# GpSimd's weight split reordered, an earlier opening, and two reorderings between TensorE and VectorE in a four-block model kernel

## What is computed

```
x = x + rmsnorm(mamba2_mixer(rmsnorm(x)))          # in-projection 1024 -> 6176, conv of 4 taps, 8 groups of
                                                   # 4 heads over 4 chunks of 128 tokens, gate, out 2048 -> 1024
x = x + rmsnorm(swa_sink_mixer(rmsnorm(x)))        # 4 key/value heads, window of 128, sinks, gate, out
x = x + conv_pool_mixer(rmsnorm(x)); x = x + swiglu_ffn(rmsnorm(x))
x = x + hgrn2_mixer(rmsnorm(x));     x = x + swiglu_ffn(rmsnorm(x))
out = rmsnorm(x)

# the part of the mamba mixer that the change touches
z, xbc, dt = split(h @ w_in)
xs, B, C   = split(silu(causal_conv(xbc)))
y = ssd(xs, dt, A, B, C) + d_skip * xs
y = rmsnorm(y * silu(z), gate_norm) @ w_out
# and of the attention mixer
o = softmax(...) @ v ;  o = (o * silu(gate)) @ w_out
```

## Time and profile before

| | |
|---|---|
| time, median of 3 runs | 1910.3 us (1908.22 to 1911.41) |
| the profiled execution | 1910.12 us |
| its span | 1908.2 us |
| TensorE busy | 1849.4 us, 97% of the span |
| VectorE, ScalarE, GpSimd busy | 1063.2, 583.2, 890.2 us |
| TensorE's mean granted clock | 0.986 of full speed |
| 16 DMA engines: the transfers into wl, the loads | 45.5%, 25.9% of their time |

### The profile page before, as it was taken

How to read it: one execution, slowest core, us unless ns; L and a number is a source line. 1 busy time by engine, 2 the same in 40 slices (tenths; PEclk the granted TensorE clock), 3 DMA queues, 4 the chain that set the end, 5 groups by cost and what they waited for, 6 DMA issues and landing times.

```text
span 1908.2 us, 25036 instructions
## 1 busy us (share of the span) xinstructions
PE 1849.4 (97%) x9691; PEld 1473.4 (77%) x9691; DVE 1063.2 (56%) x1660; ACT 583.2 (31%) x1035; POOL 890.2 (47%) x902
## 2 busy tenths in 40 slices
PE   7999999899999899999999999999999999999998
PEld 5788888687777577478888888887777788888887
DVE  6888887865778647453333321357778733333212
ACT  3444444512334322142111100136656521111001
POOL 4444445354533155245555555654332455555553
PEclk9999999999999899999999999999999999999999
DMA  8777776568555387848888888986653598888875
GB/s 209 166 151 158 150 160 145 130 160 179 124 123 118 72 187 167 202 97 190 194 194 194 194 182 191 203 188 133 133 127 85 125 200 194 194 191 198 181 173 134
DMA packets 217317, 309.92 MB, mean 162 GB/s; under 512 B 22864, under 2 KB 171504, under 8 KB 217200
## 3 DMA queue, kind: packets, MB, share of 16 engines
q0 software_dynamic: 42912, 148.65, 45.5%
q1 hardware_dynamic: 169872, 154.28, 25.9%
q10 hardware_dynamic: 4416, 5.39, 1.1%
HBM read 153.12 MB, written 2.10 MB: 81 GB/s over the span
## 4 chain that ended last, share of the span: by engine, by line
PE 87%; DVE 7%; ACT 2%; issue 2%; DMA 1%; POOL 1%; ACTq 0%; DVEq 0%; POOLq 0%
PE gp L712 22%; PE gp L714 22%; PE gp L713 22%; PE gp L657 2%; PE gp L684 2%; PE gp L658 2%; PE gp L659 2%; PE mp L978 1%; PE gp L686 1%; PE gp L685 1%; PE mp L1081 1%; DVE m_xs L1847 1%; DMA wl<-stage 1%; PE mp L852 1%; PE mp L944 1%
## 5 line engine op out<-in xcount | busy, mean ns | idle before, releaser
L605 POOL TENSOR_SCALAR wh<-stage 128x1024 fp32r<-128x1024 f32 (+3 forms) x300 | 349.3, 1164 | 900.7 <-PE gp L714 712.4
L712 PE MATMUL gp<-hh,wh 128*128 128x512 f32 x1504 | 602.8, 401 | 2.4 <-DMA wl<-stage 0.9
L713 PE MATMUL gp<-hh,wl 128*128 128x512 f32 x1504 | 587.5, 391 | 0.0
L714 PE MATMUL gp<-hl,wh 128*128 128x512 f32 x1472 | 575.8, 391 | 0.0
L611 POOL TENSOR_SCALAR wl<-stage 128x1024 fp32r<-128x1024 f32 (+2 forms) x298 | 350.8, 1177 | 0.0
L712 PEld LDWEIGHTS gp<-hh,wh 128*128 128x128 f32 x1504 | 283.3, 188 | 73.0 <-issue 12.8
L713 PEld LDWEIGHTS gp<-hh,wl 128*128 128x128 f32 x1504 | 283.7, 189 | 57.1 <-issue 1.5
L714 PEld LDWEIGHTS gp<-hl,wh 128*128 128x128 f32 x1472 | 277.3, 188 | 59.7
L614 POOL DMA_DIRECT2D wl<-stage x298 | 263.9, 886 | 94.7 <-POOL wl L611 86.4
L2262 DVE TENSOR_TENSOR val<-gp,rstd 128x512 f32<-128x512 f32 x44 | 30.4, 692 | 203.9 <-PE gp L714 203.9
L2155 DVE TENSOR_TENSOR xT<-gp,xT 128x512 f32<-128x512 f32 x31 | 21.4, 689 | 194.6 <-PE gp L714 189.7
(11 more groups left out here) (381 smaller groups left out, 2773.2 us busy)
## 6 DMA issues: line engine op xcount, KB each, us to landing
wl<-stage POOLq DMA_DIRECT2D x263, 512.0 KB, 5.2
stage<-ffn_w SPq DMA_DIRECT2D x120, 512.0 KB, 4.5
stage<-ssm_w_in SPq DMA_DIRECT2D x32, 512.0 KB, 5.0
stage<-hg_w_in SPq DMA_DIRECT2D x32, 512.0 KB, 4.5
stage<-ssm_w_in SPq DMA_DIRECT2D x32, 256.0 KB, 3.9
stage<-ssm_w_out SPq DMA_DIRECT2D x16, 512.0 KB, 4.2
stage<-att_w_in SPq DMA_DIRECT2D x14, 512.0 KB, 4.7
stage<-cp_w_in SPq DMA_DIRECT2D x12, 512.0 KB, 5.7
```

Of the source, the lines that this page charges most:

```text
L605: pool.tensor_scalar(wh[:, s, part], stage[:, s, part], 1.0, 1.0, ALU.mult, ALU.mult).then_inc(hi_done, 1)
L712: pe.matmul(bank[:, :], wvh[:, cols], hi(kk), start=start, stop=False)
L713: pe.matmul(bank[:, :], wvl[:, cols], hi(kk), start=False, stop=False)
L714: mm = pe.matmul(bank[:, :], wvh[:, cols], lo(kk), start=False, stop=stop)
```

## The change

- **GpSimd's order.** For every half after the first two: negative part, transfer, then high part (before: high part, negative part, transfer). SyncE waits also for the high part before it reloads `stage`. The first two halves are split in two pieces each. GpSimd waits for y1's low part before the first half of the out-projection's second unit.
- **Opening products.** In the LEAD units TensorE waits for the high part of tile k, runs all high products, then waits for the low part and runs the low products.
- **Opening.** The first norm rows (`pre_norm`) are waited for and turned alone; loads of x and of parameters are put later in SyncE's queue, and in two lots; x tiles are turned in another order; `sum_squares` follows the LEAD units; the second lot of parameters is turned in g = 0, slot 4 of TensorE (`turn_late`), after VectorE's copy of the skip weights, which now stands after the dt chain.
- **End of the mamba loop.** TensorE runs six granules of the out-projection ahead of slot 0 of g = 8; its list (2, 4, 4, 4, 4, 4) stays. `gate_y` of group 6 is taken apart: the read of the bank (`gate_read`) moves to the end of g = 7, behind y0's and y1's low parts, the rest (`gate_rest`) into slot 0 of g = 8, behind `mask_cb`. The last z tiles go into `raw` (`z_of`). `y_split` keeps its ranges for the slots of g = 8.
- **Attention.** `gate_o(h-1, 0)` moves from k = 8 to k = 6, behind the takes of that slot and ahead of `normalise` at k = 7.

```diff
 def rows(r0, n, src):
     eng.dma_start(prow[r0:r0 + n, 2, :], src).then_inc(norm_landed, 16)
-rows(0, 16, pre_norm.rearrange("l (t p) -> (l t) p", p=P))
+eng.dma_start(prow[0:16, 2, :], pre_norm.rearrange("l (t p) -> (l t) p", p=P)).then_inc(pre_landed, 16)
...
 load_x(0)
-load_x(1)
 for q, (u, i) in enumerate(halves):
     un, s = units[u], q % HALVES
     if q == EARLY:
+        load_x(1)
         load_x(2)
+    if q == HALVES:
         load_x(3)
-    if q == HALVES:
+    if q == HALVES + 2:
         load_parameters(sp)
+    if q == HALVES + 4:
+        load_late_parameters(sp)
     if q >= HALVES:
         if s < EARLY and q < 2 * HALVES:
-            sp.wait_ge(early_split, s + 1)
+            sp.wait_ge(early_split, 2 * (s + 1))
         else:
             sp.wait_ge(lo_landed[s], 16 * (q // HALVES - (s < EARLY)))
+            sp.wait_ge(hi_done, q - HALVES - EARLY + 1)
     ka, kb = rows_of(u, i)
     dst = stage[:, s, 0:(kb - ka) * un.cols].rearrange("p (k n) -> p k n", k=kb - ka)
...
             pool.wait_ge(gemm_part, unit_end[before])
         else:
             pool.wait_ge(first_used, before + 1)
-    pool.tensor_scalar(wh[:, s, part], stage[:, s, part], 1.0, 1.0, ALU.mult, ALU.mult).then_inc(hi_done, 1)
+        if (u, i) == (phases["ssm_out"][0] + 1, 0):
+            pool.wait_ge(split_done, split0["y"] + 2)
     if q < EARLY:
-        pool.wait_ge(hi_done, q + 1)
-        pool.tensor_tensor(wl[:, s, part], stage[:, s, part], wh[:, s, part].bitcast(F32),
-                           ALU.subtract).then_inc(early_split, 1)
+        n = (kb - ka) // 2 * un.cols
+        for piece in range(2):
+            part = slice(piece * n, (piece + 1) * n)
+            pool.tensor_scalar(wh[:, s, part], stage[:, s, part], 1.0, 1.0, ALU.mult,
+                               ALU.mult).then_inc(early_hi, 1)
+            pool.wait_ge(early_hi, 2 * q + piece + 1)
+            pool.tensor_tensor(wl[:, s, part], stage[:, s, part], wh[:, s, part].bitcast(F32),
+                               ALU.subtract).then_inc(early_split, 1)
         continue
     pool.tensor_scalar(wl[:, s, part], stage[:, s, part], -1.0, 1.0, ALU.mult,
                        ALU.mult).then_inc(neg_done, 1)
     pool.wait_ge(neg_done, q + 1 - EARLY)
     pool.dma_start(wl[:, s, part], stage[:, s, part], accum_op=ALU.add).then_inc(lo_landed[s], 16)
+    pool.tensor_scalar(wh[:, s, part], stage[:, s, part], 1.0, 1.0, ALU.mult, ALU.mult).then_inc(hi_done, 1)
...
     q = place[u, half]
-    pe.wait_ge(hi_done, q + 1)
     if q < EARLY:
-        pe.wait_ge(early_split, q + 1)
+        pe.wait_ge(early_split, 2 * q + 1)
     else:
+        pe.wait_ge(hi_done, q + 1 - EARLY)
         pe.wait_ge(lo_landed[q % HALVES], 16 * (q // HALVES + 1 - (q % HALVES < EARLY)))
...
     for k in range(KT if lead else 0):
         if ahead:
             ahead(k)
-        pe.wait_ge(split_done, split(k) + 1)
+        pe.wait_ge(hi_ready, split(k) + 1)
         if sum_early and k == KT - 1:
             after_first()
         for u in range(u0, u0 + lead):
             wvh, wvl = weights_at(u, k)
             if k in (0, KT // 2):
                 weights_whole(u, k // (KT // 2))
+            if k == KT // 4 and place[u, 0] < EARLY:
+                pe.wait_ge(early_split, 2 * place[u, 0] + 2)
             for m, t in enumerate(units[u].tiles):
                 if k == 0 and t >= 4:
...
                 pe.matmul(bank[:, :], wvl[:, cols], hi(k), start=False, stop=False)
-                mm = pe.matmul(bank[:, :], wvh[:, cols], lo(k), start=False, stop=(k == KT - 1))
+        pe.wait_ge(split_done, split(k) + 1)
+        for u in range(u0, u0 + lead):
+            wvh, _ = weights_at(u, k)
+            for m, t in enumerate(units[u].tiles):
+                cols = slice(m * P, (m + 1) * P)
+                mm = pe.matmul(gp[t % 4][:, :], wvh[:, cols], lo(k), start=False, stop=(k == KT - 1))
                 if k == KT // 2 - 1 and t == units[u].tiles[-1]:
                     mm.then_inc(first_used, 1)
...
+def turn_late():
+    pe.wait_ge(late_landed, 16 * N_LATE)
+    pe.wait_ge(skip_ready, 1)
+    pe.wait_ge(prm_ready, 2)
+    turn_rows((1, 3))
 pe.wait_ge(const_landed, 16)
+pe.wait_ge(pre_landed, 16)
+turn_pre()
 for k in range(2):
     turn_x(k)
-pe.wait_ge(norm_landed, 16 * N_NORM)
-turn_rows((2,))
-turn_x(2)
 def mamba():
-    gran = h_granules("ssm", "pre0", LEAD["ssm"], lambda: sum_squares(pre_round[0]),
-                      lambda k: turn_x(k + 3))
+    def ahead(k):
+        for j in range(2 if k > 1 else 1, 3):
+            if k:
+                turn_x(k + j)
+    gran = h_granules("ssm", "pre0", LEAD["ssm"], ahead=ahead)
     run(gran, 6)
+    sum_squares(pre_round[0])
...
     for g in range(SG + 1):
         def mix(slot):
             if g == 0:
+                if slot == 4:
+                    turn_late()
                 if slot == 5:
                     turn_dt()
...
             elif slot == 5:
                 y_tile(p, 1)
+        if g == SG:
+            run(gran_out, 6)
         for slot in range(6):
             if g < SG and (g or slot > 1):
...
             if g > 0:
                 if slot == 0:
                     copy_B(p)
+                    if g == SG:
+                        gate_square(p - 1, 0)
+                        gate_square(p - 1, 1)
                 elif slot in (1, 2):
                     for h in pair:
                         decay_between(p, h)
-                elif slot == 4:
+                elif slot == 4 and g != SG - 1:
                     gate_square(p, 0)
-                elif slot == 5:
+                elif slot == 5 and g != SG - 1:
                     gate_square(p, 1)
-            if g < SG:
-                if g == SG - 1 and slot == 5:
-                    for k in y_split[0]:
-                        high_y(k)
+            if g < SG - 1:
                 if slot >= 4:
...
-                    silu(g, slot - 2)
                 if slot == 4:
                     silu(g, 2)
+            if g < SG and 2 <= slot < 4:
+                silu(g, slot - 2)
+            if g == SG - 1 and slot == 5:
+                silu(g, 2)
+                silu_z(g, 0)
+                high_y(0)
+                high_y(1)
+                silu(g, 3)
+                silu_z(g, 1)
+                high_y(2)
+                high_y(3)
     for k in range(14, 16):
         high_y(k)
...
     dve.wait_ge(x_turned, k + 1)
     dve.tensor_copy(xT[:, k, :], mp[1 + k % 2][:, :]).then_inc(x_tile, 1)
+dve.wait_ge(prm_turned, 1)
+dve.tensor_copy(prm[:, 2 * P:2 * P + 16], mp[0][:, 2 * P:2 * P + 16]).then_inc(prm_ready, 1)
 for k in range(2):
     take_x(k)
-dve.wait_ge(prm_turned, 1)
-dve.tensor_copy(prm[:, 2 * P:3 * P], mp[0][:, 2 * P:3 * P]).then_inc(prm_ready, 1)
 for k in range(KT):
-    if k < KT - 2:
-        take_x(2 + k)
+    for j in range(0 if k == 2 else 1, 2):
+        if 1 < k < KT - 1:
+            take_x(k + j)
     low_of_x(0, k)
 dve.wait_ge(par_landed, 16 * N_PAR)
-dve.tensor_copy(prow[32:48, 3, :].rearrange("t (j d) -> t j d", j=2),
-                skip_raw[:, :].unsqueeze(2).to_broadcast([16, 2, HD])).then_inc(skip_ready, 1)
 dve.wait_ge(rstd_ready, pre_round[0] + 1)
...
         if j >= 4:
-            if g:
+            if g == SG - 1:
+                dve.wait_ge(conv_done, 4 * g + j - 1)
+            elif g:
                 dve.wait_ge(yg_ready, 2 * g - 5 + j)
-            dst = sz[:, j - 4, :]
+            dst = z_of(g, j - 4)
         else:
             if n >= 2:
...
                 step(ins)
         ins.then_inc(h_ready, 1)
-    def gate_y(g, t):
+    def gate_read(g, t):
         n = 2 * g + t
         col = P_SKIP + n
         dve.wait_ge(y_ready, n + 1)
-        dve.wait_ge(zsilu_ready, n + 1)
         if n >= 2:
             dve.wait_ge(gsq_ready, n - 1)
         v = val[:, t, :]
         dve.scalar_tensor_tensor(v, xs[:, g % 2, t, :], prm[:, col:col + 1], mp[t][:, :],
                                  ALU.mult, ALU.add).then_inc(y_read, 1)
+    def gate_rest(g, t):
+        n = 2 * g + t
+        v = val[:, t, :]
         dve.wait_ge(y_read, n + 1)
-        dve.tensor_tensor(v, v, sz[:, t, :], ALU.mult).then_inc(yg_ready, 1)
...
+    dve.wait_ge(late_landed, 16 * N_LATE)
+    dve.tensor_copy(prow[32:48, 3, :].rearrange("t (j d) -> t j d", j=2),
+                    skip_raw[:, :].unsqueeze(2).to_broadcast([16, 2, HD])).then_inc(skip_ready, 1)
     for g in range(SG + 1):
         p = g - 1
         for slot in range(6):
+            if g == 0 and slot == 5:
+                dve.wait_ge(prm_turned, 3)
+                step(dve.tensor_copy(prm[:, P:2 * P], mp[0][:, P:2 * P]))
+                dve.tensor_copy(prm[:, 3 * P:432], mp[0][:, 3 * P:432]).then_inc(prm_ready, 1)
+                dve.wait_ge(prm_ready, 3)
             if g < SG and slot < 4 and (g or slot > 1):
...
                     scale_x(p, 0)
                     scale_x(p, 1)
                     mask_cb(p)
+                    if g == SG:
```

(25 more changed lines are left out.)

60 lines of the change are left out of this document (39 added, 21 removed).

## The result

The changed kernel takes **1944.1 us** (median of 4, 1942.1 to 1951.8) against 1909.8 for the kernel before (4 runs): ratio 1.018, 95% interval 1.016 to 1.020. The forecast was 1903 with a range of 1894 to 1912. It is slower by 34 us.

The account below looks back on a forecast made before the run. The prediction took TensorE, busy 97% of the span, as the bound: its work plus its idle time. Opening -4, end of mamba loop +14.6, attention -14, everywhere -3.6 gave -7.0 on 1910.1: 1903 us, range 1894 to 1912.

Parts of the forecast that it names:

- D: Everywhere: earlier transfer into wl ends the waits for weights (2.0 us), opening products start earlier (1.6): -3.6 us (0 to -5).
- A: Opening: earlier first weight product and rstd, a shorter VectorE chain to tokT: -4 us (bounds 0 and -7).
- Rival 4: Opening gives nothing, since only VectorE's chain counts and its blocks fall worse: 1907 us; chance 0.12.
- B: End of the mamba loop: old waits go, but TensorE waits 12.2 us for y4's low part: +14.6 us (+9 to +20).
- C: Attention: earlier gate_o removes most of 12.2 us of TensorE waits and regains clock: -14 us (bounds -8 and -17).
- D's other half: Opening products in attention and conv/pool start without the low part, 0.8 us earlier each: 1.6 us gained.
- Rival 2: Slower: in the tail, VectorE's SBUF operations each meet a GpSimd burst at 1 to 3 us; above 1914 us; chance 0.09.

Follow-up runs that it names:

- e7: Kernel before with GpSimd's order negative part, high part, transfer, the transfer also waiting for the high part: 1909.8 us, ratio 1.000.
- e1: Kernel before with only GpSimd's new order (negative part, transfer, high part; SyncE also waits for the high part): 1950.8 us, ratio 1.020.
- e2: Changed kernel with GpSimd's old order (high part, negative part, transfer) for all halves but the first two: 1908.4 us, ratio 0.998.
- e5: Kernel before with only the new opening, its opening products in the new order (high parts of all tiles first): 1909.9 us, ratio 1.000.
- e12: Kernel before with the attention edit, GpSimd's order negative part, high part, transfer without a gap, and the new opening with its products: 1890.1 us, ratio 0.989.
- e11: Kernel before with the attention edit and GpSimd's order negative part, high part, transfer without a gap: 1890.2 us, ratio 0.989.
- e4: Kernel before with only the new order at the end of the mamba loop: 1922.9 us, ratio 1.005.
- e3: Kernel before with only the attention edit (gate_o moved from k = 8 to behind the rope of k = 6): 1899.5 us, ratio 0.993.
- e9: Kernel before with only the new opening, but its opening products in the old order (tile by tile): 1907.4 us, ratio 0.999.

## Why the prediction was wrong

**The step that failed is D, with what A said of GpSimd.** D priced the new order at "-3.6 us (0 to -5)", looking at who waits for the high part and for SyncE: "The high part comes later, but the transfer takes 5 us and covers it." Both were right, TensorE waits for no high part and e7 shows SyncE's wait free. It did not ask what the new sequence does to VectorE, which waits for no semaphore of GpSimd's. Measured, the order is +40.5 alone (e1) and +36 in the changed kernel (against e2). A came closest: it saw an L1693 held behind three instructions and wrote "The new order still has three in a row (transfer, high, the next negative), so I leave this cost as it is". The three in a row are the right ones. That they come 2 us earlier in the burst, in every group, was not followed beyond the opening. What D gave the wait for weights, 2.0 us, was right: e1 has no such wait.

**The margin was in no view that I used.** The list of waits shows what waits now. The 0.7 us between VectorE's read (end 279.59) and TensorE's turn (280.33) is no wait, and 2.40 us six times came out of it. The list cannot show this; only the timeline of the releaser beside that of the waiter does. (When TensorE does wait for this read it starts 0.15 us behind its end, so 0.6 us of the 0.7 were spare.)

**A, the opening** (-4, bounds 0 and -7): -5.3 at the loop by itself (e5), so the sum was right there: first product at 8.81 (I had 8.9), tokT at 67.6 (I had 69). In the changed kernel it was -1.5, since GpSimd's order falls on the same chain (tokT came at 70.3) and the first of the six waits of 2.40 stands ahead of that turn. At the end of the run the opening is 0 (e5, e12 against e11): that a gain here would be given back later is not in the prediction. Rival 4's term for the opening, nothing, was right, but not its reason: VectorE's chain was quicker.

**B, the end of the mamba loop** (+14.6, of which 12.2 for y4): the wait for y4 is 12.7 us, and the stage costs +13.9 in e2 (from -5.2 at g = 6 to +8.7 at attention), +12.5 in e4. The two waits that it put behind that one, 0.8 and 3.5 us, are 0.9 and 2.7 in e2, and 4.2 and 3.5 in the changed kernel. The low parts in the changed kernel, as counted there from L1335 on:

```profile
399.62 2.49 DVE L1999 TENSOR_TENSOR m_yl<-m_y,hh 128x512 fp32r<-128x512 f32 x4
```

The first of them ends at 400.30, 18.0 us after the turn's start at 382.30; the count had 17.3 to 18.5. The windows of that wait and behind it (columns as in the earlier trace rows) show the low level too, with a granted clock of 0.71, 0.61 and 0.50:

```profile
382.30:400.40 18.10, 5.45 (x34) 4.35 (x32) 12.30 (x19) 10.35 (x22) 5.15 (x6) 0.71 0.78 185
400.40:404.40 4.00, 3.95 (x11) 3.19 (x12) 1.71 (x3) 0.00 (x0) 0.00 (x0) 0.61 0.00 0
419.00:423.00 4.00, 3.81 (x9) 3.10 (x10) 1.85 (x4) 0.00 (x0) 0.00 (x0) 0.50 0.53 106
```

**C, attention** (-14, bounds -8 and -17): -13.9 for the stage in e3, -12.9 in e2, -9.9 in the changed kernel, where GpSimd's order lengthens `normalise` (L985 waits 3.7 us, L932 0.7 before). The term was right.

**D's other half**, 1.6 us for the opening products, is not there (e9 against e5).

So -5.3 + 13.9 - 13.9 and nothing for D would have given 1905 for the kernel with the old order of GpSimd, against the 1908.4 of e2 (which loses 3.8 in hgrn, from -3.6 to +0.2 in the starts; no step of the prediction has that, and why it does was not settled); the kernel with the new one lies 36 us above. Rival 2 is the nearest in kind (VectorE's operations under GpSimd's bursts), but it looked for them at the end of the loop alone, and priced 11 us.

The page of the Trainium skill that the prediction names, "SBUF — State Buffer", says further (Who interferes with whom) that VectorE operations with at most one SBUF input and outside the 2-port performance modes do not contend with GpSimd. The rows agree: in the burst at 278.54 L1973, which reads one of its two tensors from PSUM, took 0.73 as ever, while L1912 and L1981, with two SBUF inputs, were held. The sums of the runs do not rest on it.

## What to carry to other kernels

Before an instruction is moved on one engine, list what the engine that it can hold up does beside it (here VectorE on SBUF, which waits for no semaphore of GpSimd's), operation by operation; look for near misses there (a releaser that ends under a microsecond ahead), since the list of waits shows none. On GpSimd, do not queue a whole tensor operation directly behind a transfer's issue while VectorE has work on SBUF: a tiny operation and a wait for it cost 0.6 us of GpSimd each time and gave 12 us of 1910 here. And test each part of a change by itself: one of the four cost more than the whole change did, and the best kernels keep the cheapest of them, the moved `gate_o`.

## What the runs showed that was not expected

**A transfer's issue opens the hold.** An issue followed directly by whole tensor operations kept VectorE off SBUF for up to 3 us; the same operations without an issue ahead take turns with VectorE (no operation of either lost over 0.7 us by it in the rows above); after an issue with a column's operation behind it VectorE lost 0.2 us at most. In the kernel before 44 VectorE operations took over 1.5 us longer than the shortest of their kind. All but one, at 12.05, lie beside or behind an issue in an unbroken run of GpSimd's instructions. What in the hardware does this is not shown by these runs.

**One hold costs over 4 us, and when it comes the starts do not tell.** In e3 an issue of GpSimd started at 1493.04 and VectorE's L2406 at 1493.39; in the kernel before they started at 1506.55 and 1506.92. Rows of e3, then of the kernel before, then of e5, where the same two instructions are L631 and L2460:

```profile
1493.04 0.89 POOL L614 DMA_DIRECT2D wl<-stage  x1 [0.30 <-POOL wl L611]
...
1493.39 3.18 DVE L2406 TENSOR_TENSOR val<-val,h_g 128x512 f32<-128x512 f32 x1
```

```profile
1506.55 0.89 POOL L614 DMA_DIRECT2D wl<-stage  x1 [0.30 <-POOL wl L611]
...
1506.92 0.69 DVE L2406 TENSOR_TENSOR val<-val,h_g 128x512 f32<-128x512 f32 x1
```

```profile
1504.76 0.89 POOL L631 DMA_DIRECT2D wl<-stage  x1 [0.30 <-POOL wl L628]
...
1505.12 0.69 DVE L2460 TENSOR_TENSOR val<-val,h_g 128x512 f32<-128x512 f32 x1
```

The first is held for 2.5 us, the low part behind it (L1678, 2.59 for 0.77) as well, and TensorE waits 4.1 us for it; the other two go through. The distance of the starts does not decide it: it is 0.36 us in e3, which is held, and 0.36 in e5 and 0.37 in the kernel before, which are not; and in the changed kernel, at 707.75, an addition that started 0.37 us behind an issue took 3.17 us for 0.68. What does decide was not found. One kernel's executions here spread over 10 us and more (the kernel before 1906.5 to 1917.2 in 25 runs), and a gain of 5 us early in the program can be lost to such holds later; whether the opening's was is not shown.
